# A gather half moved behind three row groups of the first expert, and two ring rows given back one at a time

## What is computed

```python
def moe_ffn(t, router_w, router_b, w_gate, w_up, b_gate, b_up, w_down, b_down):
    logits = (t @ router_w + router_b).astype(jnp.float32)
    top_v, top_i = lax.top_k(logits, TOP_K)
    gates = jax.nn.softmax(top_v, axis=-1)
    ...
    def expert_block(inp):
        tok, gt, e = inp
        xb = t_pad[tok]
        hid = clamped_swiglu(xb @ w_gate[e] + b_gate[e], xb @ w_up[e] + b_up[e])
        yb = hid @ w_down[e] + b_down[e]
        return (yb * gt[:, None].astype(yb.dtype)).astype(t.dtype)
```

## Time and profile before

| | us |
|---|---|
| median of 3 runs | 1055.86 |
| lowest and highest of them | 1055.48 and 1057.0 |
| profiled execution | 1056.45 |
| its span, first to last instruction | 1054.6 |
| PE busy in it | 1019.8 |

### The profile page before, as it was taken

The page is one execution under the profiler, slowest core; times in us unless marked ns, Lnnn a source line. Parts: engine busy times, 40 slices in busy tenths (PEclk is TensorE's granted clock), DMA queues, the critical chain, the costliest instruction groups (busy, mean ns, idle before and its releaser), DMA issues.

```text
span 1054.6 us, 12382 instructions
## 1 busy us (share of the span) xinstructions
PE 1019.8 (97%) x5112; PEld 450.7 (43%) x5112; DVE 236.4 (22%) x562; ACT 149.9 (14%) x381; POOL 30.8 (3%) x51
## 2 busy tenths in 40 slices
PE   8999999999999999999999999999999999999998
PEld 7888764333333333332333333333333333323332
DVE  5453661211111111111111112211111111111113
ACT  3312331111111111100111011111111110101102
POOL 2230100000000000000000000000000000000000
PEclk9999999999999999999999999999999999999999
DMA  9895879999999999999999999999999999999995
GB/s 315 269 410 200 274 308 400 430 434 426 432 434 427 431 434 431 430 434 434 430 430 435 429 417 430 428 436 428 429 431 432 434 429 434 431 428 427 426 418 234
DMA packets 40589, 426.22 MB, mean 404 GB/s; under 512 B 6986, under 2 KB 19411, under 8 KB 24036
## 3 DMA queue, kind: packets, MB, share of 16 engines
q1 hardware_dynamic: 38516, 424.12, 95.9%
q10 hardware_dynamic: 2032, 1.53, 0.6%
HBM read 424.59 MB, written 1.05 MB: 404 GB/s over the span
## 4 chain that ended last, share of the span: by engine, by line
PE 74%; DMA 23%; SPq 2%; DVE 0%; ACT 0%; issue 0%; POOL 0%; POOLq 0%; DVEq 0%
PE bank L1250 32%; PE bank L1312 16%; DMA ring<-in_moe_w_up 15%; DMA ring<-in_moe_w_gate 5%; PE bank L1230 5%; PE bank L1207 5%; PE bank L890 3%; DMA ring<-in_moe_w_down 2%; PE bank L905 2%; PE bank L1080 2%; SPq L441 2%; PE bank L1068 1%; PE bank L1022 1%; PE bank L1222 1%; PE bank L1154 1%; PE bank L1215 1%
## 5 line engine op out<-in xcount | busy, mean ns | idle before, releaser
L1250 PE MATMUL bank<-ring,arena 128*64 128x512 f32 x1980 | 445.5, 602 | 25.5 <-DMA ring<-in_moe_w_up 24.9
L1250 PEld LDWEIGHTS bank<-ring,arena 128*64 128x64 f32 x1980 | 142.4, 139 | 308.4 <-issue 260.9
L1312 PE MATMUL bank<-ring,arena 128*64 128x512 f32 x1024 | 227.2, 595 | 0.4 <-DMA ring<-in_moe_w_down 0.4
L1312 PEld LDWEIGHTS bank<-ring,arena 128*64 128x64 f32 x1024 | 70.6, 137 | 133.3 <-issue 130.8
L1721 DVE COPY arena<-bank 128x512 f32<-128x512 f32 x32 | 22.1, 691 | 326.5 <-PE bank L1312 326.5
L762 ACT ACTIVATE arena<-arena 128x512 f32<-128x512 f32 x32 | 20.1, 630 | 418.1 <-DVE arena L1704 418.1
L1230 PE MATMUL bank<-arena 64*128 64x512 f32 x256 | 72.0, 640 | 0.9 <-DVE arena L1721 0.9
L1715 DVE TENSOR_SCALAR arena<-bank 128x256 f32<-128x256 f32 x64 | 26.9, 420 | 203.0 <-PE bank L1250 203.0
L1207 PEld LDWEIGHTS bank<-arena 128*128 128x128 f32 x480 | 59.0, 196 | 22.8 <-issue 22.8
L780 ACT ACTIVATE arena<-bank 128x256 f32<-128x256 f32 x64 | 21.4, 381 | 329.4 <-PE bank L1222 329.4
L1207 PE MATMUL bank<-arena 128*128 128x128 f32 x480 | 64.9, 288 | 0.0
(11 more groups left out here) (286 smaller groups left out, 517.5 us busy)
## 6 DMA issues: line engine op xcount, KB each, us to landing
ring<-in_moe_w_down SPq DMA_DIRECT2D x25, 4096.0 KB, 27.7
ring<-in_moe_w_gate SPq DMA_DIRECT2D x24, 4096.0 KB, 23.6
ring<-in_moe_w_up SPq DMA_DIRECT2D x24, 4096.0 KB, 26.4
ring<-in_moe_w_down SPq DMA_DIRECT2D x10, 2048.0 KB, 15.5
ring<-in_moe_w_gate SPq DMA_DIRECT2D x9, 2048.0 KB, 21.8
ring<-in_moe_w_up SPq DMA_DIRECT2D x9, 2048.0 KB, 14.2
ring<-in_w_in SPq DMA_DIRECT2D x12, 1024.0 KB, 11.7
ring<-in_moe_w_gate SPq DMA_DIRECT2D x8, 1024.0 KB, 16.4
```

Of the source, the lines that this page charges most:

```text
L1250: ins = mm(b[h * SL:(h + 1) * SL, :], (xA[pp], xB)[q][:, k, par * SL:(par + 1) * SL], columns(unit_at(m, kt), h), start=False, stop=kt == ...
L1312: ins = mm(bank[6][h * SL:(h + 1) * SL, :], hidT[:, kt % 4, (kt // 4) * SL:(kt // 4 + 1) * SL], unit_at(2, kt)[:, h * 512:(h + 1) * 512], ...
```

## The change

Four things are done, all of them for expert 0's gate matrix.

1. Block 1 of gather half 1 (four matmuls) is taken from its place ahead of the first row group and put between the third and the fourth row group (kt 2 and kt 3).
2. The row groups kt 4 to 7 no longer wait together for all four copies of half 1. ACT raises `xT_row` after each of the first three, and each row group waits for its own. (`xT_dve` and `mixT_dve` are renamed to `xT_row` and `mixT_row`, since two engines raise them now.)
3. Rows 2 and 3 of slot 0 are given back and reloaded one by one, in place of one piece of two rows. So slot 0 is reloaded in six pieces, and the counts of the later pieces go up by one.
4. The new piece has the landing semaphore `w_landed8`, so the wait of the last expert that uses the same one counts to 48 in place of 32.

```diff
-FIRST_PIECES = ((0, 1, 2, 4, 6, 7), (0, 2, 4, 6, 7), (0, 2, 4, 6, 8))
-FIRST_USED = (1, 5, 8, 11)
-FIRST_LANDED = ({1: 11, 2: 0, 6: 1}, {2: 2, 6: 3}, {2: 4, 6: 5})
+FIRST_PIECES = ((0, 1, 2, 3, 4, 6, 7), (0, 2, 4, 6, 7), (0, 2, 4, 6, 8))
+FIRST_USED = (1, 6, 9, 12)
+FIRST_LANDED = ({1: 11, 2: 0, 3: 8, 6: 1}, {2: 2, 6: 3}, {2: 4, 6: 5})
...
+                    if each and k < 3:
+                        ins.then_inc(xT_row, 1)
...
-            xT_evac(1, 1, bank[6], xB, None)
+            xT_evac(1, 1, bank[6], xB, None, each=True)
...
-            for half, banks in enumerate((half0, half1)):
-                gather_part(1, half, banks).then_inc(gath_ps, 1)
+            gather_part(1, 0, half0).then_inc(gath_ps, 1)
...
-                            if first and m == 0 and k == 0:
-                                pe.wait_ge(xT_ok, q + 1)
-                                pe.wait_ge(xT_dve, 1)
+                            if first and m == 0 and kt == 0:
+                                pe.wait_ge(xT_ok, 1)
+                                pe.wait_ge(xT_row, 1)
+                            if first and m == 0 and kt == 3:
+                                gather_part(1, 1, half1).then_inc(gath_ps, 1)
+                            if first and m == 0 and kt >= 4:
+                                pe.wait_ge(*((xT_row, kt - 2) if kt < 7 else (xT_ok, 2)))
...
-                            pe.wait_ge(w_landed[u], 48 if u < 8 else 32)
+                            pe.wait_ge(w_landed[u], 48 if u < 9 else 32)
```

More of the change, by code:

```diff
@@ L253, in build @@
         y_mid, ssq, rms_in, rms, mix_y, o_ok, mix_o = sem("y_mid"), sem("ssq"), sem("rms_in"), sem("rms"), sem("mix_y"), sem("o_ok"), sem("mix_o")
-        mixT_ps, mixT_act, mixT_dve, wout_ps = sem("mixT_ps"), sem("mixT_act"), sem("mixT_dve"), sem("wout_ps")
+        mixT_ps, mixT_act, mixT_row, wout_ps = sem("mixT_ps"), sem("mixT_act"), sem("mixT_row"), sem("wout_ps")
         var1, rstd1, rstd_ok, cen, h1p_ok, cg_ok, bdn_ok = (sem("var1"), sem("rstd1"), sem("rstd_ok"), sem("cen"), sem("h1p_ok"), sem("cg_ok"),
@@ L259, in build @@
                                                                 sem("GT_ps"), sem("GT_ok"))
-        count_ps, sel0_ok, oh_ok, xT_dve = sem("count_ps"), sem("sel0_ok"), sem("oh_ok"), sem("xT_dve")
+        count_ps, sel0_ok, oh_ok, xT_row = sem("count_ps"), sem("sel0_ok"), sem("oh_ok"), sem("xT_row")
         tables_ok, bparts_ok, list_ok = sem("tables_ok"), sem("bparts_ok"), sem("list_ok")
@@ L748, in _, with xT_evac @@
             act.wait_ge(ln1_in, 48)
-            def xT_evac(g, half, b, dst, done, upto=4):
+            def xT_evac(g, half, b, dst, done, upto=4, each=False):
                 act.wait_ge(gath_ps, g + 1)
@@ L1128, in _ @@
             pe.wait_ge(mixT_act, 3)
-            pe.wait_ge(mixT_dve, 1)
+            pe.wait_ge(mixT_row, 1)
             for nb in range(2):
@@ L1579, in _ @@
                     dve.wait_ge(mixT_ps, 4)
-                    copy(mixO[:, 2:4, :].rearrange("p a n -> p (a n)"), bank[7][:, :]).then_inc(mixT_dve, 1)
+                    copy(mixO[:, 2:4, :].rearrange("p a n -> p (a n)"), bank[7][:, :]).then_inc(mixT_row, 1)
                 ins = copy(bparts[0:n, :, :], braw[0:n, :, :])
@@ L1651, in _ @@
                 ins = ts(xA[0][:, k, :], bank[5][:, k * P:(k + 1) * P], gq[:, 0, k:k + 1], bq[:, 0, k:k + 1], ALU.mult, ALU.add)
-            ins.then_inc(xT_dve, 1)
+            ins.then_inc(xT_row, 1)
             link(nc.vector.reciprocal(gsum, gsum))
```

## The result

The changed kernel takes 1057.56 us (median of 21 runs, 1056.73 to 1058.86) against 1055.88 us for the kernel before on the same chips (21 runs, 1054.93 to 1057.98). The sum had said 1056.0. The profiled execution took 1057.56 us, with a span of 1055.8.

What follows compares the result with a forecast made beforehand. The prediction took the unbroken DMA stream of weights as the bound. Start 0, PE's 1.02 us off the path, stream 0, split +0.1 and last expert's count 0 on 1055.86 gave 1056.0 us, range 1054.9 to 1057.6.

Steps and rivals of the forecast that it cites:

- The sum: Whole kernel: all terms added to the kernel before's median of 1055.86 us, +0.1, giving 1056.0 us.
- Rival B: Weight stream breaks in expert 0, at slot 2's second piece and rows 3 to 5; at most 1057.1 us; chance 0.10.
- A: Weight stream is not broken in expert 0; -0.2 to +0.4, 1055.7 to 1056.3 us; chance 0.74.
- The start gains 0: Expert 0's first row group starts when it did, as PE waits 1.24 us for the copies; gain 0.
- ACT and DVE cost 0: In expert 0, ACT's later copies and table load and DVE's later select and weigh delay nothing; 0 us.
- No wait ahead of row group 4: Expert 0's gate matrix: half 1's first copy is ready when PE gets there; 0, bounds 0 and 0.1 us.
- C: PE's clock falls within row groups 0 to 3 after the idle stretch; 1057.6 to 1058.5 us; chance 0.03.
- PE loses 1.02 us: The moved gather block delays PE from row group 3 of expert 0's gate matrix on, by 1.02 us.
- The split +0.1: Reloading rows 2 and 3 of slot 0 as two DMAs costs the weight stream 0.1 us.
- Every reserve, 1.2 to 3.1 us, is larger than the lateness: Expert 0's reloads could each be issued 1.2 to 3.1 us later, so 1.02 us of lateness moves no landing.
- seven reserves: Lateness that expert 0's reloads and the first whole matrix could bear, from landing times; 1.2 to 3.1 us.

Runs made afterwards that it cites:

- e3: The kernel before plus four extra 128x128 matmuls ahead of row group 3 of expert 0's gate matrix; 1056.77 us, ratio 1.0011.
- e2: The kernel before with only the split added, rows 2 and 3 of slot 0 given back one by one; 1055.95 us, ratio 0.9997.
- e1: The changed kernel with rows 2 and 3 of slot 0 reloaded in one piece again; 1057.07 us, ratio 1.0012.
- e4: The kernel before plus four extra 128x128 matmuls ahead of row group 0 of expert 0's up matrix; 1057.30 us, ratio 1.0012.
- e9: The kernel before with selection transposes and last gather chunk moved behind row group 5 of expert 0's down matrix; 1055.96 us, ratio 0.9999.
- e10: The kernel before without three of sixteen matmuls of expert 0's gate matrix (second half of row groups 4 to 6); 1055.84 us, ratio 0.9999.
- e11: The kernel before plus eight extra 128x128 matmuls ahead of expert 28's up matrix; 1059.15 us, ratio 1.0021.

## Why the prediction was right or wrong

**The total** came out inside the range and within the 0.2%, but not for my reason. Rival B gives 1057.1 at most, the measured median is 1057.56. I had put 0.74 on A and 0.10 on B. That the range held is luck: its upper end of 1057.6 lies 0.04 us above the result, and it doesn't follow from my own words, as B's 1057.1 with the 1.1 us of spread would be 1058.2. B had its place nearly right (row 3 and slot 2), but not its first condition (a lateness over 1.5 us; it was 1.3) and not its price (1.22 us; it was 1.7). Its second condition, a lone 1 MB over 5.4 us, no run tested.

**The start gains 0**: right, 155.79 against 155.77. **ACT and DVE cost 0**: right, the copies end at 161.26 and the table load at 162.56. **No wait ahead of row group 4**: right. **C**, the falling clock, didn't come where I had put it: the granted clock is 1.00 in all windows from 154 to 186 us, behind an idle stretch of 1.16 us.

**PE loses 1.02 us**: too small by 0.3. I multiplied 8 records by the 0.128 that one takes in a row of 24. A block of 8 between matmuls of another shape takes 1.28 from the row ahead to the row behind. e3's eight records of the same size take 1.24 (row group 0 at 155.84, row group 3 at 159.66). So each of the two changes of shape costs PE a little over 0.1 us, and a mean from a long block doesn't hold it.

**The split +0.1**: measured at 0.0, with the interval of e2.

**Every reserve, 1.2 to 3.1 us, is larger than the lateness**: this step failed, and with it the forecast. I took the time of a lone DMA from the time of each piece, and called the rest standing behind others, by which the piece could be late. Two things were wrong in it. First, the time to landing is no queue: in the changed kernel slot 2's pieces find about 0.1 MB less ahead of them and take 7.1 and 7.0 us where they took 6.6 and 6.4. Nor was the DMA at 151.88, my price for 1 MB, alone: in 151 to 152 us the engines were busy with a share of 0.92. Second, being busy is no pace: the windows of 158 to 170 us of the kernel before moved 334, 364 and 399 GB/s with shares of 0.94 to 1.01. That the stream was below its pace there stood in the trace, and so did a second hole, of which I had made nothing:

```profile
164.00:165.00 1.00, 1.00 (x6) 0.34 (x4) 0.69 (x1) 0.25 (x1) 0.00 (x0) 1.00 0.70 254
```

In windows of 30 us from 166 on neither can be seen. What the runs showed in place of the reserves: row 3 and slot 2's first piece had none, slot 1's first piece 0.3 to 0.9 us. 1.3 us of lateness gave 1.0 to 1.9 us in the stream at 433 us and 0.9 to 2.1 at the last landing (e1, e3, e4, the changed kernel), 2.1 to 2.3 gave 2.8 and 3.2.

I named a possible reason under B ("the 16 engines need not finish alike") and gave it 0.10, because it stood against seven reserves that agreed. But all seven came from one subtraction. They were one piece of evidence. The wider spread of the 16 landing counts (2.3 and 2.7 us in place of 1.5) fits that reason; that it is the cause isn't shown.

**What stays open.** Whether a microsecond of lateness costs more than one isn't settled: the stream's shift says up to 1.6, the medians of e1, e3, e4 and the changed kernel say 0.8 to 1.7 for 1.3. Nor is it shown what makes a transfer slow while the engine counts as busy. The amount of data issued and not yet moved doesn't tell it: worked out from issues and packets, it is 2.3 to 2.8 MB when the changed kernel moves 338 GB/s at 170 to 172 us, 2.2 to 1.3 MB when the kernel before moves 438 at 172 to 174, and 1.5 MB in the hole at 164 to 165. And the loss is not always kept. In e3 slot 2's pieces land 2.5 us late, while at 433 us the shift is 1.0; e1's shift falls from 1.9 at 433 us to 0.9 at the last landing. How the stream makes that up isn't shown.

## What to carry to other kernels

Read the pace of a stream in GB/s over short windows, and not as busy share. A reserve is shown by delaying the stage: four extra matmuls in front of it answered in one run what a subtraction of landing times had answered wrongly. Earliness and lateness are not opposites: where the stream ran at full pace, pieces issued 0.95 us earlier landed no sooner (e9), and pieces issued 1.3 us later landed up to 2.0 us later (e4). And see in the trace that an experiment's edit did what it was for before reading its time: e10's time said that earliness brings nothing, but its edit had made nothing earlier.

## What the hardware showed that I had not expected

With a share of 0.99 to 1.02 the 16 DMA engines moved anything from 346 to 428 GB/s in windows of 4 us. Two matmuls of 128x64 by 128x512 that write the two halves of a bank's partitions ran side by side, so that leaving out one of the two saved nothing (e10). Eight more matmuls in a stage where PE waits for data anyway cost 2.8 us (e11), all of it in the last 17 us of the kernel, where a stop of 1.44 us and a clock at the lower level followed. The same final four records took 1.88 us at a granted clock of 1.00 and 3.51 at 0.55 in executions of kernels that don't differ in that place. Among the kernel before's own runs, which spread over 3 us, that could by this account for some 1 us, which is an estimate.
